# Token axis split at 256, the second token half of the first four weight groups first, in a hybrid decoder step on one core

## The chip, the cores and the metric

One Trainium2 chip, of which the kernel uses one core. The metric is the device time of one execution in microseconds (us). The core has TensorE (PE; its weight loads are PEld), VectorE (DVE), ScalarE (ACT), GpSimd (POOL) and SyncE (SP), which issues most of the DMAs. Each engine works its own instruction list in order and waits on semaphores.

## The reference

One layer of a hybrid decoder for a prompt of 512 tokens and 8 single-token samples (520 tokens in all), in float32:

```python
xn = rmsnorm(x, ln1_w)
z = xn @ w_in          # 1024 -> 3592 columns: q, k, v of attention; q, k, v, gate of mLSTM; 8 gate columns
attn = moba_attention(qa, k_all, v_all, q_start)     # 8 heads x 64; samples look at 1024 cached tokens
h, C, n, m = mlstm_chunkwise(qm, km, vm, i_pre, f_pre, C0, n0, m0)   # 4 heads x 128, matrix memory
mix = concat(attn, rmsnorm(h) * sigmoid(om))
x = x + mix @ w_out
x = x + square(relu(rmsnorm(x, ln2_w) @ w_up)) @ w_down              # 1024 -> 4096 -> 1024
y = rmsnorm(x, lnf_w)
```

Outputs are y, the new keys and values, and the mLSTM states, for prompt and samples.

## The kernel before

Activations lie transposed: features on the 128 partitions, the 520 tokens along the free axis. Each large product is made of three products of a high and a low part (`w_hi*x_hi + w_hi*x_lo + w_lo*x_hi`), summed in PSUM. A weight group is 128 output columns, 1024 deep. Its raw weights come by DMA into `raw` (two slots, a "unit" of two groups each, on SP's queue), ACT rounds them to `w_hi` (`split`, L1096), and DVE or POOL makes `w_lo` (`weight_lo`, L1103). Four groups fit in `w_hi` and `w_lo`. The token axis is cut in two halves of 260. A group and a half make one slot: 24 matmuls of 260 columns into one of three accumulators, which DVE evacuates (`evac_copy`, L1953) with the norm's factor `rstd1`. PE may start slot i only when slot i-3 has been evacuated. Slots 0 to 55 are the 28 input groups, 56 to 71 the 8 output groups; then follow 64 MLP groups.

What else has to be done is written by hand into the slots: `plan()` puts named tasks behind each slot, and each engine does its part of slot s and of the slot's tasks before it goes on to s+1. The tasks that matter here:

- `gates`: 24 matmuls for the gate columns of one half; `rows`, `rows_f`, `rows_sum`, `rows_max`, `rows_M`, `rows_s`, `rows_end`, `gcols` (slots 4 to 11): the running sums and maxima of the gates, on 4 partitions, most of it on DVE.
- `qs_tok`, `qb` (slots 8 and 9): the samples' queries, copied to all partitions as `Qb`.
- `score`: 32 chunks of cached keys. POOL multiplies a chunk of two pages with `Qb` (`prod`, two buffers, L1476), DVE reduces it to `S` (L1655). Chunk n stands in slot `10 + (2n+1)//3`, so in slots 10 to 31; key pages for chunk n+4 are issued on SP when chunk n is multiplied.
- `gate`, `mx_t`, `own`, `mx_b`, `p_sum`, `zsum` (slots 32 to 36), then `pv` from slot 37: the choice of blocks, softmax and the product with the cached values.
- `att_*`: prompt attention; `ml_*`: mLSTM. `ml_m` of head 0 stands in slot 27: ACT writes `mA`, POOL masks it (L1510).

At the start SP issues the four token tiles, unit 0, the gate columns, the page table, unit 1 and small loads, waits until the last token tile has been transposed and squared, issues 8 key pages (they lie over the token tiles), and only then unit 2. PE transposes all four tiles (32 transposes, L742), ACT and DVE split them at 512 columns (`act_hi` L1153, `act_lo` L1564), and slot 0 begins. POOL makes `w_lo` of groups 0 to 2, DVE of groups 3 to 19: group n in the even slot 2(n-3), ahead of that slot's evacuation.

Of the kernel before, what the change touches and what calls it, by code (L numbers as in the profile page):

```python
# [24 lines left out]
ALU = mybir.AluOpType  # L25
# [13 lines left out]
HALF = TOK // 2  # L39
# [34 lines left out]
HALVES = [(g, half) for g in range(N_IN) for half in range(2)]  # L74
# [11 lines left out]
def z_ready(g):  # L86

    return 2 * (g + 1)
# [19 lines left out]
def chunk_slot(n):  # L108

    return 10 + (2 * n + 1) // 3  # L110


def pv_slot(b):

    return 37 + 12 * b // 5
# [5 lines left out]
def plan():  # L121
# [6 lines left out]
    at(2, ("gates", 0))  # L128
    at(3, ("gates", 1))
    at(4, ("rows",))  # L130
    at(5, ("rows_f",))
    at(6, ("rows_sum",))
    at(7, ("rows_max",))
    at(8, ("qs_tok",), ("rows_M",))
    at(9, ("qb", 0), ("qb", 1), ("rows_s",))
    at(10, ("rows_end",))
    at(11, ("gcols",))
# [13 lines left out]
    at(32, ("gate",))  # L151
    at(33, ("mx_t",), ("own",))
    at(34, ("mx_b",))
    at(35, ("p_sum",))
    at(36, ("zsum",))
    for b in range(4):
        at(36, ("s_put", b))
# [9 lines left out]
    at(pv_slot(7) + 3, ("pv_end",))  # L167
    for h in range(MH):
# [12 lines left out]
        at((52, 54, 55, 55)[h], ("om_mix", h))  # L181
# [17 lines left out]
    for n in range(4 * NS):  # L199
        at(chunk_slot(n), ("score", *divmod(n, 4)))  # L200
        if n % 4 == 1 and n >= 5:
            at(chunk_slot(n), ("qb", n // 4 + 1)) if n // 4 + 1 < NS else None
    for t in range(4):
# [3 lines left out]
        "gates": 1, "gcols": 1, "qs_tok": 1, "qb": 1, "vs_tok": 1, "tokk": 1, "tokv": 1, "tokm": 2,  # L207
# [10 lines left out]
    for j in range(4, KT):  # L218
        job("xn", j)
    job("par2", 0)  # L220
    job("rstd1", 0)
    job("rstd1", 1)
# [29 lines left out]
def build(nc, x_prompt, x_sample, cache_k, cache_v, page_table, state_C, state_n, state_m, ln1_w, w_in,  # L252
# [4 lines left out]
    with ctx:  # L257
# [37 lines left out]
        mix, _ = place("mix", [P, N_IN, TOK], F32R, at=z_at)  # L295
        x_sq, _ = place("x_sq", [P, 2, TOK], at=z_slot(VA))
# [111 lines left out]
        s_pt_in = sem("pt_in")  # L408
        s_raw0 = sem("raw0")
# [17 lines left out]
        s_x_acc = sem("x_acc")  # L427
        s_x_lo = sem("x_lo")
# [130 lines left out]
        def _(sp):  # L559
            for i in range(NT):  # L560
                sp.dma_start(x_tok[:, i, :], x_prompt[0, i * P:(i + 1) * P, :]).then_inc(x_in[i], 16)
# [20 lines left out]
            unit(0)  # L582
# [3 lines left out]
            unit(1)  # L586
# [4 lines left out]
            full(sp, "xn", KT - 1)  # L591
            sp.wait_ge(s_x_sq_ok, NT + 1)
# [55 lines left out]
        def _(pe):  # L648
# [8 lines left out]
            def token_half(half):  # L657
                return slice(half * HALF, (half + 1) * HALF)

            def half_gemm(i, parts, k_ready=None):  # L660

                g, half = HALVES[i]
                pe.wait_ge(s_w_lo_ok, g + 1)
                if i >= 3:
                    pe.wait_ge(s_acc_evac, i - 2)
                for k in range(KT):
                    if k_ready is not None:
                        k_ready(k)
                    three(acc[:, i % 3, 0:HALF], g % WSLOTS, parts, token_half(half), k, k)

            def main(g, slot, side, parts, k_ready=None, between=None):
# [3 lines left out]
                def part(half, k):  # L675
                    three(acc[:, 2 * side + half, 0:HALF], slot, parts, token_half(half), k, k)
# [43 lines left out]

            pe.wait_ge(s_ident_ok, 3)

            for i in range(NT):
                pe.wait_ge(x_in[i], 16)
                if i == 2:

                    out = open_job(pe, "param", 0)
                    pe.wait_ge(s_ln1_in, 16)
                    pe.transpose(out[:, 0:KT], ln1_rows[:, :], ident[0:KT, 0:KT])
                    pe.wait_ge(x_in[NT], 16)  # L730
                    for j in range(KT):
                        mm = pe.transpose(out[:, 32 + j * NS:32 + (j + 1) * NS], x_s[:, j * P:(j + 1) * P],
                                          ident[0:NS, 0:NS])
                    done(mm)
                for j in range(KT):
                    if j == 7 and i < 2:
                        continue
                    out = acc[:, j, :] if j < 4 else bank("xn", j)
                    if j == 7 and i == 2:
                        open_job(pe, "xn", j)  # L740
                    for n in range(3) if j == 7 and i == 2 else (i,):
                        mm = pe.transpose(out[:, n * P:(n + 1) * P], x_tok[:, n, j * P:(j + 1) * P], ident[:, :])  # L742
                    if i == NT - 1 and j < 4:
                        mm.then_inc(s_x_acc, 1)
                    elif i == NT - 1:
                        done(mm)

            def task(name, *a):
                if name == "gates":
                    half, = a  # L750
                    if half == 0:
                        pe.wait_ge(s_wg_lo_ok, 2)
                    cols = token_half(half)
                    out = open_job(pe, "gates", half, 0)[:, 0:HALF]
# [14 lines left out]
                elif name == "qs_tok":  # L769
                    pe.wait_ge(s_acc_evac, z_ready(QA + 3))  # L770
# [263 lines left out]
            for i in range(N_HALVES):  # L1034
                if i == 0:
                    half_gemm(i, x_parts, x_split)
                    pe.wait_ge(s_xs_ok, 1)
                elif i < 2 * N_IN:
# [49 lines left out]
        def weight_hi(act, g, slot, r_slot, target):  # L1088

            act.wait_ge(raw_in[r_slot], target)  # L1090
# [17 lines left out]
        def _(act):  # L1108
# [34 lines left out]
            square_sum(1)  # L1143
            split(0)
            act.wait_ge(s_par_ok, 1)

            for j in range(KT):
                if j < 4:
                    act.wait_ge(s_x_acc, j + 1)
                    out = acc[:, j, :]  # L1150
                else:
                    out = full(act, "xn", j)
                act.activation(act_hi[:, j, 0:SEQ], out, ACT.Copy, scale=par[:, j:j + 1]).then_inc(s_xhi_ok, 1)  # L1153
                if j == 5:
                    split(1)
            square_sum(2)
            square_sum(NT - 1)
            split(2)
            free(act.activation(par[:, KT:20], full(act, "par2", 0)[:, 0:KT + MH], ACT.Copy), "par2", 0)
# [13 lines left out]
            def task(name, *a):  # L1173
                if name == "rows_f":
# [28 lines left out]
                elif name == "va_s":  # L1203
                    act.wait_ge(s_smp_out, 16)
# [223 lines left out]
        def _(pool):  # L1428
# [22 lines left out]
            for rows_split in (qs_split, M_split):  # L1451
                pool.memset(rows_split[:, :].bitcast(F32), 0.0).then_inc(s_sel_ok, 1)
            pool.memset(vm_tok[:, :, MD:MD + 1], 1.0).then_inc(s_vm_ones, 1)
            weight_lo(pool, 0, 0, 0)
            weight_lo(pool, 1, 1, 0)
            pool.wait_ge(s_x_ms_ok, 2)
            rsqrt(rs[:, 0:NT], P, NT).then_inc(s_x_rs_ok, 1)
            rsqrt(rs[0:NS, NT:NT + 1], NS, 1).then_inc(s_x_rs_ok, 1)
# [5 lines left out]
                               ALU.subtract).then_inc(s_wg_lo_ok, 1)  # L1464

# [51 lines left out]
            for s in range(N_HALVES):  # L1517
                n = s // 2 + AHEAD
                if s % 2 == 0 and n >= POOL_LO:
# [22 lines left out]
        def _(dve):  # L1542
# [16 lines left out]

            dve.wait_ge(s_par_ok, 1)  # L1560
            for j in range(KT):
                dve.wait_ge(s_xhi_ok, j + 1)
                out = acc[:, j, :] if j < 4 else full(dve, "xn", j)
                ins = dve.scalar_tensor_tensor(out=act_lo[:, j, 0:SEQ], in0=out, scalar=par[:, j:j + 1],  # L1564
                                               in1=act_hi[:, j, 0:SEQ].bitcast(F32), op0=ALU.mult, op1=ALU.subtract)
                if j < 4:
                    ins.then_inc(s_x_lo, 1)
                else:
                    free(ins, "xn", j)

# [6 lines left out]

            dve.wait_ge(s_x_sq_ok, NT + 1)
# [503 lines left out]
```

## Time and profile before

| what | us |
|---|---|
| median of 3 runs | 761.29 |
| lowest, highest | 758.21, 764.3 |
| profiled execution, its time | 758.09 |
| profiled execution, its span | 756.4 |

The span is that of the instructions; the time has 1.7 us around it. Working back from a row of the trace gives times within the span of the profiled execution, which is near the lowest of the three runs.

### The profile page before, as it was taken

To read this page: it belongs to the slowest core of one execution; us is meant where nothing else is said; L and a number is where in the kernel's file an instruction comes from. 1 tells how busy PE (TensorE), PEld (TensorE's weight loads), DVE (VectorE), ACT (ScalarE), POOL (GpSimd) and SP (SyncE) were. 2 spreads that over 40 slices of the span, in tenths; PEclk is the share of its full clock that TensorE was granted. 3 is DMA by queue.
4 is the path that set the end of the run, shared out by engine and by line. 5 is a ranking of instruction groups with operands and counts; after the bars stand their busy time and mean duration, and the time that the engine had idled before them with its cause. 6 is when DMAs were issued, how large, how long until landed. Compare 5 with 4: busy or idle time off the path is not lost.

```text
span 756.4 us, 14650 instructions
## 1 busy us (share of the span) xinstructions
PE 717.1 (95%) x5709; PEld 666.4 (88%) x5709; DVE 360.4 (48%) x649; ACT 254.9 (34%) x428; POOL 213.3 (28%) x154
## 2 busy tenths in 40 slices
PE   6999889698999999899999999999999999999995
PEld 5988778576968776599999999999999999999994
DVE  3279778768543346345334433334334333333333
ACT  6233645434452222215333311342223321233123
POOL 4207987743223253163222100220002200022001
PEclk9999999899999999999999999999999999999998
DMA  7627988654356868723123332232331331322102
GB/s 226 200 81 170 287 271 255 186 158 129 98 161 209 265 194 162 263 85 113 56 70 103 109 112 79 90 111 68 100 112 55 111 111 57 110 84 85 58 1 113
DMA packets 93732, 100.37 MB, mean 133 GB/s; under 512 B 5358, under 2 KB 75586, under 8 KB 93674
## 3 DMA queue, kind: packets, MB, share of 16 engines
q1 hardware_dynamic: 79670, 92.91, 39.8%
q10 hardware_dynamic: 14004, 6.67, 3.3%
q8 instruction: 39, 0.64, 0.4%
q14 instruction: 19, 0.16, 0.1%
HBM read 92.92 MB, written 6.64 MB: 132 GB/s over the span
## 4 chain that ended last, share of the span: by engine, by line
PE 74%; DVE 8%; issue 4%; DMA 4%; ACT 4%; POOL 4%; SPq 1%; ACTq 0%; POOLq 0%; DVEq 0%
PE acc L651 22%; PE acc L652 21%; PE acc L653 21%; DMA raw<-in_w_in_dram 2%; PE acc L932 2%; DMA kv<-in_cache_v_dram 2%; DVE w_lo L1103 2%; POOL prod L1476 1%; PE scr L982 1%; ACT w_hi L1096 1%; PE scr L863 1%; DVE S L1655 1%; PE scr L876 1%; PE scr L957 1%; DVE zT L1953 1%
## 5 line engine op out<-in xcount | busy, mean ns | idle before, releaser
L651 PE MATMUL acc<-act_hi,w_hi 128*128 128x260 f32 x960 | 277.8, 289 | 4.6 <-POOL w_lo L1103 2.6
L652 PE MATMUL acc<-act_lo,w_hi 128*128 128x260 f32 x960 | 273.1, 285 | 0.0
L653 PE MATMUL acc<-act_hi,w_lo 128*128 128x260 f32 x960 | 272.8, 284 | 0.0
L651 PEld LDWEIGHTS acc<-act_hi,w_hi 128*128 128x128 f32 x960 | 182.9, 191 | 12.4 <-issue 6.6
L653 PEld LDWEIGHTS acc<-act_hi,w_lo 128*128 128x128 f32 x960 | 183.0, 191 | 0.0
L652 PEld LDWEIGHTS acc<-act_lo,w_hi 128*128 128x128 f32 x960 | 183.0, 191 | 0.0
L1096 ACT ACTIVATE w_hi<-raw 128x1024 fp32r<-128x1024 f32 x100 | 105.2, 1053 | 185.0 <-PE acc L653 167.6
L1103 DVE TENSOR_TENSOR w_lo<-raw,w_hi 128x1024 fp32r<-128x1024 f32 x78 | 111.7, 1432 | 108.3 <-ACT w_hi L1096 107.9
L651 PE MATMUL acc<-h_hi,w_hi 128*128 128x260 f32 x512 | 144.6, 282 | 0.0
L652 PE MATMUL acc<-h_lo,w_hi 128*128 128x260 f32 x512 | 144.6, 282 | 0.0
L653 PE MATMUL acc<-h_hi,w_lo 128*128 128x260 f32 x512 | 144.4, 282 | 0.0
L1533 POOL TENSOR_TENSOR h_lo<-relu,h_hi 128x520 fp32r<-128x520 f32 x32 | 42.0, 1313 | 275.8 <-ACT h_hi L1404 275.8
L653 PEld LDWEIGHTS acc<-h_hi,w_lo 128*128 128x128 f32 x512 | 96.5, 188 | 0.0
L652 PEld LDWEIGHTS acc<-h_lo,w_hi 128*128 128x128 f32 x512 | 96.4, 188 | 0.0
L651 PEld LDWEIGHTS acc<-h_hi,w_hi 128*128 128x128 f32 x512 | 96.3, 188 | 0.0
L1476 POOL TENSOR_TENSOR prod<-kv,Qb 128x1024 f32<-128x1024 f32 x32 | 82.0, 2586 | 49.9 <-ACT Qb L1168 33.2
L1103 POOL TENSOR_TENSOR w_lo<-raw,w_hi 128x1024 fp32r<-128x1024 f32 x22 | 52.7, 2395 | 105.5 <-ACT w_hi L1096 105.5
L1973 DVE TENSOR_TENSOR xT<-acc,xT 128x260 f32<-128x260 f32 x64 | 27.1, 428 | 90.0 <-PE acc L653 90.0
L1403 ACT ACTIVATE relu<-relu 128x520 f32<-128x520 f32 x32 | 20.4, 639 | 123.5 <-DVE relu L2023 123.5
L1953 DVE TENSOR_TENSOR zT<-acc,rstd 128x260 f32<-128x260 f32 x56 | 23.5, 422 | 50.2 <-PE acc L653 47.4
L2023 DVE SCALAR_TENSOR_TENSOR relu<-acc,rstd 128x260 f32<-128x260 f32 x64 | 26.7, 422 | 39.1 <-PE acc L653 39.1
L1655 DVE TENSOR_REDUCE S<-prod 128x16 f32<-128x1024 f32 x32 | 38.3, 1209 | 8.4 <-POOL prod L1476 8.4
(294 smaller groups left out, 777.3 us busy)
## 6 DMA issues: line engine op xcount, KB each, us to landing
kv<-in_cache_k_dram SPq DMA_DIRECT2D x64, 256.0 KB, 3.2
kv<-in_cache_v_dram SPq DMA_DIRECT2D x64, 256.0 KB, 3.0
raw<-in_w_up_dram SPq DMA_DIRECT2D x16, 1024.0 KB, 5.4
raw<-in_w_down_dram SPq DMA_DIRECT2D x16, 1024.0 KB, 5.2
raw<-in_w_in_dram SPq DMA_DIRECT2D x8, 1024.0 KB, 6.2
raw<-in_w_in_dram SPq DMA_DIRECT2D x12, 512.0 KB, 5.4
x_tok<-in_x_prompt_dram SPq DMA_DIRECT2D x8, 512.0 KB, 5.2
raw<-in_w_out_dram SPq DMA_DIRECT2D x4, 1024.0 KB, 6.0
```

The lines of the kernel that those rows point to most:

```text
L651: pe.matmul(out, w_hi[:, slot, k, :], hi[k][:, cols], start=(n == 0), stop=False)
L652: pe.matmul(out, w_hi[:, slot, k, :], lo[k][:, cols], start=False, stop=False)
L653: mm = pe.matmul(out, w_lo[:, slot, k, :], hi[k][:, cols], start=False, stop=(n == KT - 1))
L1096: act.activation(w_hi[:, slot, :, :], raw[:, r_slot, :, side * P:(side + 1) * P], ACT.Copy)\
L1103: eng.tensor_tensor(w_lo[:, slot, :, :], raw[:, r_slot, :, side * P:(side + 1) * P], w_hi[:, slot, :, :].bitcast(F32), ALU.subtract).then_ ...
L1403: act.activation(relu2[:, t % 2, :], relu[:, t % 2, :], ACT.Square)
L1476: pool.tensor_tensor(prod[:, n % 2, :].rearrange("p (j n) -> p j n", j=2), kv[:, 2 * c:2 * c + 2, :], Qb[:, b % 2:b % 2 + 1, :].to_broadca ...
L1533: pool.tensor_tensor(h_lo[:, t, :], relu2[:, t % 2, :], h_hi[:, t, :].bitcast(F32), ALU.subtract).then_inc(s_hs_lo, 1)
L1655: dve.tensor_reduce(S[:, b, 2 * c:2 * c + 2, :].rearrange("p j h -> p (j h)"), prod[:, n % 2, :].rearrange("p (g d) -> p g d", d=AD), AX.X ...
L1953: dve.tensor_tensor(zT[:, g, cols], acc[:, i % 3, 0:HALF], rstd1[:, cols], ALU.mult)\
L1973: dve.tensor_tensor(x, acc[:, 2 * side + half, 0:HALF], x, ALU.add).then_inc(s_acc_evac, 1)
L2023: dve.scalar_tensor_tensor(out=relu[:, t % 2, cols], in0=acc[:, 2 * (t % 2) + half, 0:HALF], scalar=0.0, in1=rstd2[:, cols], op0=ALU.max, ...
```

## The change

The halves are now tokens 0 to 255 and tokens 256 to 519 (256 and 264 columns). The first eight slots are half 1 of groups 0 to 3, then half 0 of groups 0 to 3; from slot 8 on the order is as before. Token tiles 2 and 3 are loaded first, then group 0 and group 1 each in a DMA of its own, then tiles 0 and 1, then unit 1; gate columns, page table and small loads come behind it. Tiles 0 and 1 are transposed, split and squared as tasks of slots 1 and 2. In its first four slots PE waits for `w_lo` only after the 16 matmuls that need `w_hi` alone. The samples' square sum goes from ACT to DVE, the copy `va_smp` from DVE to ACT. The weights of groups 4 to 7 are split in slots 5 to 8; POOL makes `w_lo` of group 3 too. `qs_tok` and `qb` stand in slots 4 and 5, the `rows` tasks in slots 6 to 12, key scoring in slots 6 to 29, ahead of the `ml` tasks of the same slot, and `gate` to `zsum` and all `pv` one slot earlier.

```diff
-HALVES = [(g, half) for g in range(N_IN) for half in range(2)]
+HALVES = [(g, half) for half in (1, 0) for g in range(WSLOTS)]
+HALVES += [(g, half) for g in range(WSLOTS, N_IN) for half in range(2)]
...
+def token_half(half):
+    return slice(SPLIT_TOK, TOK) if half else slice(0, SPLIT_TOK)
...
+def split_at(s):
+
+    if s < 2 * WSLOTS + 1:
+        return s - 1 if s > WSLOTS else None
+    n = s // 2 + AHEAD
+    return n if s % 2 == 0 and n >= 2 * WSLOTS else None
...
 def chunk_slot(n):
 
-    return 10 + (2 * n + 1) // 3
+    return 6 + 3 * n // 4
...
 def pv_slot(b):
 
-    return 37 + 12 * b // 5
+    return 36 + 12 * b // 5
...
+    at(0, ("par2",), ("rstd", 1))
+    at(1, ("xn", 0), ("xn", 1))
+    at(2, ("xn", 2), ("xn", 3), ("square", 0), ("square", 1))
+    at(3, ("gates", 1), ("rstd", 0))
+    at(4, ("qs_tok",))
+    at(5, ("gates", 0), ("qb", 0), ("qb", 1))
+    at(6, ("rows_f",))
+    at(7, ("rows_sum",))
+    at(8, ("rows_max",))
+    at(9, ("rows_M",))
+    at(10, ("rows_s",))
+    at(11, ("rows_end",))
+    at(12, ("gcols",))
...
-            unit(0)
+            tokens(2)
+            tokens(3)
+            for n in range(2):
+                sp.dma_start(raw[:, 0, :, n * P:(n + 1) * P],
+                             w_in[0, :, COL[n] * P:(COL[n] + 1) * P].rearrange("(k p) n -> p k n", p=P))\
+                  .then_inc(raw_in[0] if n else s_raw_first, 16)
+            tokens(0)
+            tokens(1)
+            unit(1)
...
             sp.wait_ge(s_pt_in, 16)
-            full(sp, "xn", KT - 1)
-            sp.wait_ge(s_x_sq_ok, NT + 1)
+            full(sp, "xn", 3, 0)
+            sp.wait_ge(s_x_sq_ok, NT)
             for j in range(PAGES):
                 page(cache_k, 0, j)
...
+                if i < WSLOTS:
+                    hi, lo = parts
+                    pe.wait_ge(s_w_hi_ok, g + 1)
+                    for k in range(KT):
+                        pe.matmul(out, w_hi[:, g, k, :], hi[k][:, cols], start=(k == 0), stop=False)
+                        pe.matmul(out, w_hi[:, g, k, :], lo[k][:, cols], start=False, stop=False)
+                    pe.wait_ge(s_w_lo_ok, g + 1)
...
+            square_sum(2)
...
+            square_sum(3)
+            act.wait_ge(s_par_ok, 1)
+            x_hi(("x1", 0), 0, 1)
+            x_hi(("x1", 1), 1, 1)
             split(0)
+            x_hi(("x1", 2), 2, 1)
+            x_hi(("x1", 3), 3, 1)
+            split(1)
             split(2)
...
+                elif name == "xn":
+                    n, = a
+                    if n == 2:
+                        split(3)
+                    x_hi(("xn", n, 0), n, 0)
+                elif name == "square":
+                    square_sum(*a)
...
             for s in range(N_HALVES):
-                n = s // 2 + AHEAD
-                if s % 2 == 0 and n < POOL_LO:
-                    if n == AHEAD:
-                        dve.wait_ge(s_w_lo_ok, AHEAD)
+                n = split_at(s)
+                if n is not None and n < POOL_LO:
+                    if n == WSLOTS:
+                        dve.wait_ge(s_w_lo_ok, WSLOTS)
                     weight_lo(dve, n, n % WSLOTS, n // 2 % 2)
+                if s == slot_of(0, 1):
+                    rstd_to_cols(1)
+                if s == slot_of(0, 0):
+                    rstd_to_cols(0)
```

## Rows read from the trace of the kernel before

**Rows 1.** The page: busy time, share of the span and instructions of each engine

```profile
PE 717.1 (95%) x5709; PEld 666.4 (88%) x5709; DVE 360.4 (48%) x649; ACT 254.9 (34%) x428; POOL 213.3 (28%) x154
```

**Rows 2.** The waits of PE: engine, line waited for, total us, times, longest

```profile
PE scr L863 <- DVE pT_b L1901: 6.2, 1, 6.2
...
PE scr L903 <- DVE page_max L1799: 2.4, 1, 2.4
```

**Rows 3.** Busy time by stretch: PE, PEld, DVE, ACT, POOL, granted clock, DMA

```profile
140.00:160.00 20.00, 12.63 (x77) 10.64 (x75) 14.06 (x18) 2.11 (x3) 16.15 (x7) 0.83 0.61 186
...
384.00:756.00 372.00, 363.20 (x3041) 362.34 (x3040) 143.18 (x211) 107.56 (x149) 44.74 (x37) 0.99 0.27 88
```

**Rows 4.** The timeline of the start: start us, duration us, what, idle before it

```profile
2.71 0.59 SPq L573 DMA_DIRECT2D raw<-in_w_in_dram  x1
...
4.66 1.06 ACT L1135 ACTIVATE junk<-x_tok 128x1024 f32<-128x1024 f32 x1 [0.90 <-DMA x_tok<-in_x_prompt_dram]
...
6.29 1.06 PE L742 MATMUL acc<-ident,x_tok 128*128 128x128 f32 x4
...
12.04 1.06 ACT L1096 ACTIVATE w_hi<-raw 128x1024 fp32r<-128x1024 f32 x1 [1.63 <-DMA raw<-in_w_in_dram]
13.00 2.41 ACT L1153 ACTIVATE act_hi<-acc,par 128x512 fp32r<-128x512 f32 x4
13.18 2.35 POOL L1103 TENSOR_TENSOR w_lo<-raw,w_hi 128x1024 fp32r<-128x1024 f32 x1 [7.99 <-ACT w_hi L1096]
...
15.58 0.39 PE L651 MATMUL acc<-act_hi,w_hi 128*128 128x260 f32 x1 [2.59 <-POOL w_lo L1103]
```

**Rows 5.** The timeline of SP, and of ACT: key pages, units 2 and 3, groups 4 and 5

```profile
22.00 8.67 SPq L580 DMA_DIRECT2D kv<-in_cache_k_dram  x8
30.72 1.06 SPq L573 DMA_DIRECT2D raw<-in_w_in_dram  x2
...
38.12 2.01 ACT L1096 ACTIVATE w_hi<-raw 128x1024 fp32r<-128x1024 f32 x2 [12.46 <-DMA raw<-in_w_in_dram]
```

**Rows 6.** The timeline of DVE from group 4 to the evacuation of slot 13

```profile
39.21 1.22 DVE L1103 TENSOR_TENSOR w_lo<-raw,w_hi 128x1024 fp32r<-128x1024 f32 x1 [11.44 <-ACT w_hi L1096]
...
49.46 1.22 DVE L1103 TENSOR_TENSOR w_lo<-raw,w_hi 128x1024 fp32r<-128x1024 f32 x1 [2.84 <-ACT w_hi L1096]
...
59.62 2.02 DVE L1636 TENSOR_TENSOR s_rows<-rows,m_row 4x8 f32<-4x8 f32 x1
...
69.45 1.22 DVE L1655 TENSOR_REDUCE S<-prod 128x16 f32<-128x1024 f32 x1 [1.04 <-POOL prod L1476]
...
74.24 0.41 DVE L1953 TENSOR_TENSOR zT<-acc,rstd 128x260 f32<-128x260 f32 x1
```

**Rows 7.** The tile w_lo on DVE, by stretch: busy us (instructions)

```profile
38.00:64.00 26.00, 4.89 (x4) 1.00 0.33 103
66.00:160.00 94.00, 19.95 (x10) 0.95 0.83 239
```

**Rows 8.** The timeline of POOL, first key product and around head 0's masking

```profile
58.73 5.24 POOL L1476 TENSOR_TENSOR prod<-kv,Qb 128x1024 f32<-128x1024 f32 x2 [33.17 <-ACT Qb L1168]
...
138.34 1.04 POOL L1510 TENSOR_SCALAR_AFFINE_SELECT mA<-mA 128x128 f32<-128x128 f32 x4 [3.00 <-ACT mA L1281]
139.34 10.26 POOL L1476 TENSOR_TENSOR prod<-kv,Qb 128x1024 f32<-128x1024 f32 x4
```

**Rows 9.** PE by stretch: slots 0 and 1; slots 12, 13; slots 29, 30

```profile
15.58:23.73 8.15, 7.80 (x49) 0.79 0.08 21
65.09:71.12 6.03, 6.03 (x53) 1.00 0.90 116
149.54:156.97 7.43, 7.43 (x52) 0.79 0.91 300
```

**Rows 10.** The timeline of DVE in slots 25 and 27

```profile
129.41 2.24 DVE L1659 COPY va_smp<-zT 128x32 f32<-128x32 f32 x1
...
141.74 1.22 DVE L1655 TENSOR_REDUCE S<-prod 128x16 f32<-128x1024 f32 x1 [3.06 <-POOL prod L1476]
```

More of the change, by code:

```diff
@@ L38 @@
 TOK = SEQ + NS
-HALF = TOK // 2
+SPLIT_TOK = SEQ // 2
 AH, AD = 8, 64
@@ L150, in plan @@
     at(46, ("states", 4))
[L151 to L155, printed above, removed]
+    at(31, ("gate",))
+    at(32, ("mx_t",), ("own",))
+    at(33, ("mx_b",))
+    at(34, ("p_sum",))
+    at(35, ("zsum",))
     for b in range(4):
-        at(36, ("s_put", b))
+        at(35, ("s_put", b))
     for b in range(NS):
@@ L167, in plan @@
     at(pv_slot(7) + 3, ("pv_end",))
+    for n in range(4 * NS):
+        at(chunk_slot(n), ("score", *divmod(n, 4)))
+        if n % 4 == 1 and n >= 5:
+            at(chunk_slot(n), ("qb", n // 4 + 1)) if n // 4 + 1 < NS else None
     for h in range(MH):
@@ L217, in plan @@
     job("param", 0)
[L218 to L222, printed above, removed]
+    for n in range(4):
+        job("x1", n)
     for names in tasks:
@@ L559, in _, with tokens @@
         def _(sp):
-            for i in range(NT):
+            def tokens(i):
                 sp.dma_start(x_tok[:, i, :], x_prompt[0, i * P:(i + 1) * P, :]).then_inc(x_in[i], 16)
@@ L668, in half_gemm @@
                         k_ready(k)
-                    three(acc[:, i % 3, 0:HALF], g % WSLOTS, parts, token_half(half), k, k)
+                    three(out, g % WSLOTS, parts, cols, k, k)
             def main(g, slot, side, parts, k_ready=None, between=None):
@@ L675, in part @@
                 def part(half, k):
-                    three(acc[:, 2 * side + half, 0:HALF], slot, parts, token_half(half), k, k)
+                    three(acc[:, 2 * side + half, 0:width(half)], slot, parts, token_half(half), k, k)
                 def bank_free(half):
@@ L748, in task, with x_to_cols @@
-            def task(name, *a):
-                if name == "gates":
+            def x_to_cols(key, n, tiles):
+                out = open_job(pe, *key)
+                for j in (2 * n, 2 * n + 1):
+                    for c, i in enumerate(tiles):
+                        pe.wait_ge(x_in[i], 16)
+                        col = (j % 2) * SPLIT_TOK + c * P
+                        mm = pe.transpose(out[:, col:col + P], x_tok[:, i, j * P:(j + 1) * P], ident[:, :])
+                done(mm)
+            pe.wait_ge(s_ident_ok, 3)
@@ new lines, in _, with x_split_1 @@
+            out = open_job(pe, "param", 0)
+            pe.wait_ge(s_ln1_in, 16)
+            pe.transpose(out[:, 0:KT], ln1_rows[:, :], ident[0:KT, 0:KT])
+            pe.wait_ge(x_in[NT], 16)
+            for j in range(KT):
+                mm = pe.transpose(out[:, 32 + j * NS:32 + (j + 1) * NS], x_s[:, j * P:(j + 1) * P],
+                                  ident[0:NS, 0:NS])
+            done(mm)
+            for n in range(4):
+                x_to_cols(("x1", n), n, (2, 3))
+            def x_split_1(k):
+                evacuated(pe, "x1", k // 2)
@@ new lines, in x_split_0, with task @@
+            def x_split_0(k):
+                evacuated(pe, "xn", k // 2, 0)
+            def task(name, *a):
+                if name == "par2":
+                    pe.wait_ge(s_par_in, 32)
+                    out = open_job(pe, "par2", 0)
+                    done(pe.transpose(out[:, 0:KT + MH], par_rows[:, :], ident[0:KT + MH, 0:KT + MH]))
+                elif name == "rstd":
+                    half, = a
+                    pe.wait_ge(s_x_rs_ok, 2 if half else 3)
+                    out = open_job(pe, "rstd", half, 0)
+                    for n, c in enumerate((2, 3, NT) if half else (0, 1)):
+                        m = P if c < NT else NS
+                        mm = pe.matmul(out[:, n * P:n * P + m], every(rs[0:m, c:c + 1], m),
+                                       ident[0:m, 0:m], start=True, stop=True)
+                    done(mm)
+                elif name == "xn":
+                    n, = a
+                    x_to_cols(("xn", n, 0), n, (0, 1))
+                elif name == "gates":
@@ L750, in task @@
                     half, = a
-                    if half == 0:
+                    if half == 1:
                         pe.wait_ge(s_wg_lo_ok, 2)
+                    else:
+                        for k in range(KT):
+                            x_split_0(k)
                     cols = token_half(half)
-                    out = open_job(pe, "gates", half, 0)[:, 0:HALF]
+                    out = open_job(pe, "gates", half, 0)[:, 0:width(half)]
                     for k in range(KT):
@@ L1088, in weight_hi @@
         def weight_hi(act, g, slot, r_slot, target):
-            act.wait_ge(raw_in[r_slot], target)
+            if isinstance(g, int) and g == 0:
+                act.wait_ge(s_raw_first, 16)
+            else:
+                act.wait_ge(raw_in[r_slot], target)
             if not isinstance(g, int) or g >= G_MLP:
@@ L1558, in _ @@
                .then_inc(s_sel_ok, 1)
+            dve.wait_ge(x_in[NT], 16)
+            link(dve.tensor_tensor(xs_sq[:, :], x_s[:, :], x_s[:, :], ALU.mult))
+            link(dve.tensor_reduce(ss[0:NS, NT:NT + 1], xs_sq[:, :], AX.X, ALU.add))
             dve.wait_ge(s_par_ok, 1)
[L1561 to L1569, printed above, removed]
             evacuated(dve, "param", 0)
```

204 lines of the change are left out of this document (92 added, 112 removed).

## The prediction

> **What bounds the kernel now.** The page first: PE is busy 717.1 of 756.4 us, every other engine under half [rows 1]. The order of the MLP phase is not touched, and its 372 us are PE from end to end [rows 3]. So a gain can only come out of PE's idle and slowed time ahead of it. The list of PE's waits then shows that one wait is long, 6.2 us for a copy on DVE, and one of 2.4 for the block choice [rows 2]; the wait for the first tokens and weights is the third place: the first real matmul starts at 15.58 [rows 4]. The stretch 140 to 160 shows what the long wait costs beyond itself: PE busy 12.63 of 20 us at a granted clock of 0.83 [rows 3]. Slots 29 and 30 took 7.43 us at a clock of 0.79, slots 12 and 13 took 6.03 at 1.00 [rows 9], so 1.4 us more were lost to the lower level (1.2 GHz for part of the time) after PE had idled. From 6.03 us a slot is 3.0 us.
>
> **The first matmul.** Before, ACT had to wait for unit 0 until 12.04, behind four token tiles [rows 4]. Now ACT squares tile 2 from 4.66 to 5.9 (1.06 and the read of its sum), copies the parameters until 6.3, squares tile 3 until 7.6 (the tile that came second was in use at 6.29), and makes four pieces of `act_hi`. At 512 columns one takes 0.60 (2.41 for four); 256 columns lie between 0.30 and 0.60, I take 0.4, since fixed cost stays: 9.2. `w_hi` of group 0 takes 1.06: 10.2. Its weights need 1.5 MB of the 3.1 that had landed by 12.04, so they are there at about 7 to 8. First matmul 10.3 instead of 15.58, 5.3 earlier. POOL's `w_lo` (2.35) is ready at 12.6 and no longer holds the first 16 matmuls; slot 0 ends near 13.9. The samples' square sum costs DVE two operations over 1024 elements, about 1.2 each as the one that reduces 1024 [rows 6]; DVE has nothing else before the first `act_hi`, so I price it at nothing, 2.4 if that cover goes.
>
> **What is given back at once: transposes and the key pages.** Half of the transposes (16, four in 1.06 [rows 4]) move behind the first matmul. Slot 1 runs from about 14.7 to 17.7, eight transposes to 19.8, slot 2 to 22.8, eight more to 24.9. ACT then has its last pieces and two squares of 1.25: 28. SP waits for these squares before it issues key pages; with transposes somewhat faster I take 27.5, where before it was 22.00 [rows 5]; bounds 26 and 30 (the latter if the clock is low again, as in slots 0 and 1, 8.15 us at 0.79 [rows 9]). Unit 2 is queued behind the eight pages, and group 4's `w_hi` started 16.1 us after the first page (38.12 less 22.00). So it starts at 43.6, and `w_lo` of group 4 ends at 45.9, not 40.4. Slots 3 to 7, the gates (24 matmuls, as a slot), `qs_tok` and `qb` bring PE to slot 8 at about 47.8, so PE itself is not held. What is late is DVE: this `w_lo` stands ahead of its evacuation of slot 5.
>
> **The DVE chain to slot 13.** Before, from the end of `w_lo` of group 4 (40.4) to the end of slot 13's evacuation (74.65) it took 34.2 us [rows 6]. Taken away: idle time of 2.84 and 1.04; three evacuations of 0.41 (slots 2 to 4 are done by then); the gate products of one half, 0.8. Added: by the formula ten chunks instead of four stand in slots up to 12, six reductions of 1.22, 7.3. Then there is blocking. A `w_lo` on DVE took 1.22 where POOL was nearly idle (4.89 for 4) and 2.0 where POOL multiplied keys (19.95 for 10) [rows 7]; an operation on 32 elements took 2.02 just when the first two key products ran [rows 6, 8]. Four early `w_lo` and seven `rows` operations with two inputs in SBUF now stand beside key products. At 0.8 each that is 8.8, of which before had paid about 4 in `rows_s`; as the products stop whenever DVE is late, I take 2, bounds 0 and 9. Sum: 34.2 - 3.9 - 1.2 - 0.8 + 7.3 + 2 = 37.6, so slot 13 is evacuated at 83.5, 9 later. PE had slack there: slot 13 ended at 71.12 [rows 9], and slot 16, which must wait for this evacuation, had slots 14 and 15 (6.0) and tasks (I estimate 5) before it, so began near 82. It now begins at 83.5 at best and, since slots 14 and 15 are held in the same way, I take +4, bounds -2 and +9. The 5.3 us of the start are gone by then; what is kept is a lead of six chunks.
>
> **Slots 16 to 27.** Sixteen chunks where eighteen stood: 2.4 us less on DVE; and the copy of `va_smp`, 2.24 on DVE [rows 10], goes to ACT. PE waits only for part of that: -1.5, bounds 0 and -4.6.
>
> **Slots 27 to 32.** Here the lead pays. Before, seven chunks stood behind head 0's masking on POOL; POOL waited 3.00 for ACT's `mA` and then had four products back to back, 10.26 [rows 8]. DVE waited 3.06 for one of them [rows 10] with the copy behind it for which PE waited 6.2 [rows 2]. Now chunks 28 and 29 stand ahead of the masking and only 30 and 31 behind it. Wait and slow clock make 7.6; I take -7, bounds 0 and -9. The 2.4 for the block choice stays: `gate` and `mx_t` are still one slot apart.
>
> **The rest.** The cached values one slot earlier meet fewer state stores: -0.5, bounds -2 and +2. Evacuations and matmuls of 256 and 264 columns make 520 as before, so I price them at nothing; the MLP phase too.
>
> **Sum.** +4 - 1.5 - 7 - 0.5 = -5.0. The profiled execution took 758.1, so 753.1 by it; it lies 3.2 under the median of the three runs, 761.29, to which the forecast is made: 756.
>
> **The rivals.** (a) The start is kept: pages at 26, no added blocking, slot 16 two us earlier, then -1.5, -7.6 and -0.5, together -12: 749. For it: POOL was idle for 33.17 us before the first product [rows 8], and DVE's chain had 3.9 idle. Against it: DVE's sum above. (b) The wait of 6.2 is not removed but meets the next thing late, the `mA` products on DVE, which now stand behind chunk 30, itself behind the masking: +4 - 1.5 - 0.5 and nothing back, 763. For it: POOL's wait for ACT is untouched. (c) Slower: on DVE and POOL the early chunks and the `rows` chain take turns. The eleven operations each wait for the rest of a product, on average half of 2.4, 13 us less the 4 paid before, 9 at slot 16; a low clock costs 1.4 more, and of the later 7 only 2 come back, since PE arrives there with DVE late: +9 + 1.4 - 1.5 - 2 = +7, 768. It decides once slot 13's evacuation ends after about 88. For it: rows 7; against it: two product buffers let POOL run only two chunks ahead of DVE.
>
> The Trainium skill has a rule for (c): SBUF — State Buffer, section "Who interferes with whom", says that a DVE instruction with two SBUF inputs and a GpSimd instruction that reads SBUF exclude each other, the later one waiting until the first is through. The trace agrees in direction: the doubled `w_lo` and the 2.02 us for 32 elements. Taken strictly it makes every one of those operations wait, which is rival (c), 768, where my sum takes 2 us. The same section lets a reduction, with its single input, run beside POOL, and the reductions of 1.22 [rows 6] bear that out.
>
> **Chances.** Forecast 0.45, (a) 0.20, (b) 0.14, (c) 0.21. Leaving out the outer parts of (a) and (c), the range is 746 to 768. One per cent, about what a measurement of this kernel can tell from no change, is 7.6 us: faster than 753.7 is (a) and the lower third of the forecast, 0.34; slower than 768.9 the most of (c) with its spread, 0.20; between them 0.46.
>
> **What would show it.** First L651 matmul near 10.3 (wrong if over 12). First key page near 27.5, group 4's `w_hi` near 43.6. First key product near 42 instead of 58.73. `w_lo` on DVE near 2 us already before 60. Slot 13's evacuation between 79 and 88. After slot 27 no PE wait over 3 us for the copy into `pT_b`, and granted clock 1.00 there. The forecast is wrong if the early waits of PE (slots 8 to 14) add up to over 14 us, or if the pages start before 25 and DVE keeps pace.

## The result, and the profile after

The changed kernel takes 777.10 us (median of 4 runs, 776.04 to 779.11), the kernel before 760.18 (4 runs): ratio 1.022, interval 1.019 to 1.024. It is 2.2% slower, where 756 was forecast with a range up to 768. The profiled execution took 779.11 us, 777.4 of them span. It is the slowest of its four, and the profiled execution of the kernel before lies just under the fastest of its four, so the spans lie 21.0 us apart where the medians lie 16.9 apart: rows show where the time went, ratios how much it is.

The page of the changed kernel, busy line (it answers to [rows 1]):

```profile
PE 722.6 (93%) x5709; PEld 671.8 (86%) x5709; DVE 367.2 (47%) x658; ACT 254.3 (33%) x435; POOL 219.6 (28%) x156
```

The number of PE's instructions is the same as before. The span is 21.0 us longer and PE's busy time only 5.5, so 15.5 us are idle time of PE. The waits of PE name where (engine, what for, total, times, longest):

```profile
PE acc L676 <- DVE zT L2031: 10.5, 4, 5.2
PE scr L921 <- DVE pT_b L1979: 4.5, 1, 4.5
...
PE scr L967 <- DVE nmax L1961: 3.5, 1, 3.5
...
PE scr L774 <- DMA x_s<-in_x_sample_dram: 2.4, 1, 2.4
```

Against [rows 2] the first row is new: a half group waits for the evacuation (`zT`) of an earlier one, on DVE. The wait for `pT_b` is 4.5 instead of 6.2. In place of the 2.4 for the block choice stands one of 3.5. By stretch (us, then busy time of PE, PEld, DVE, ACT and POOL, granted clock, DMA share, GB/s):

```profile
40.00:60.00 20.00, 14.44 (x106) 13.40 (x106) 14.68 (x15) 7.43 (x9) 11.54 (x4) 0.89 0.69 221
60.00:80.00 20.00, 11.83 (x84) 10.88 (x83) 19.79 (x17) 3.46 (x4) 10.57 (x5) 0.84 0.45 146
...
180.00:200.00 20.00, 15.64 (x90) 13.15 (x89) 14.29 (x42) 6.40 (x16) 2.96 (x5) 0.83 0.25 66
```

Before, PE was busy 17.61 and 20.00 us in the first two of these stretches, at a granted clock of 1.00; DVE, with 19.79 of 20 us, is what it now waits for. Both stretches also lost some clock (0.89 and 0.84) after PE had idled: slots 10 and 13 took 4.8 us each instead of 3.1 and 3.0.

Where the time came from can be followed slot by slot. A slot is 24 matmuls of the query groups, so every 24th of these matmuls in the record begins one (there are 200, slots 0 to 199):

```
first matmul of slot   0      9      13     16     28     29     33     60     198
before (us)          15.58  53.74  68.08  82.26 136.27 149.54 175.47 333.39 738.65
after (us)           11.82  49.81  79.30  97.92 151.92 164.03 194.18 352.50 759.60
difference            -3.8   -3.9  +11.2  +15.7  +15.7  +14.5  +18.7  +19.1  +21.0
```

Between slots 9 and 16, 20 us are lost. All that comes later changes this by 5.

SP's and ACT's timelines, which answer to [rows 5] (start, duration, what, idle before it):

```profile
29.39 8.13 SPq L598 DMA_DIRECT2D kv<-in_cache_k_dram  x8
37.56 12.13 SPq L591 DMA_DIRECT2D raw<-in_w_in_dram  x3
```

```profile
43.58 1.06 ACT L1147 ACTIVATE w_hi<-raw 128x1024 fp32r<-128x1024 f32 x1 [8.45 <-DMA raw<-in_w_in_dram]
44.54 1.07 ACT L1216 ACTIVATE Qb<-scr 128x512 f32<-128x512 f32 x2
```

Group 4's `w_hi` came at 43.58, as forecast (43.6). The failure is in DVE's timeline from there to slot 13's evacuation, the answer to [rows 6]:

```profile
44.74 1.23 DVE L1154 TENSOR_TENSOR w_lo<-raw,w_hi 128x1024 fp32r<-128x1024 f32 x1 [8.83 <-ACT w_hi L1147]
45.88 0.42 DVE L2031 TENSOR_TENSOR zT<-acc,rstd 128x256 f32<-128x256 f32 x1
...
47.08 2.22 DVE L1154 TENSOR_TENSOR w_lo<-raw,w_hi 128x1024 fp32r<-128x1024 f32 x1
...
49.67 2.14 DVE L1685 TENSOR_SCALAR rows<-rows,bias_f 4x520 f32<-4x520 f32 x1
...
56.13 2.10 DVE L1154 TENSOR_TENSOR w_lo<-raw,w_hi 128x1024 fp32r<-128x1024 f32 x1 [0.38 <-ACT w_hi L1147]
58.16 0.41 DVE L2031 TENSOR_TENSOR zT<-acc,rstd 128x256 f32<-128x256 f32 x1
58.49 2.52 DVE L1693 SCALAR_TENSOR_TENSOR rows<-rows 4x520 f32<-4x520 f32 x1
...
62.30 1.22 DVE L1734 TENSOR_REDUCE S<-prod 128x16 f32<-128x1024 f32 x1
...
64.90 2.53 DVE L1699 TENSOR_TENSOR rows<-rows 4x512 f32<-4x512 f32 x1
...
70.19 2.58 DVE L1706 CAST M_split<-rows 4x512 fp32r<-4x512 f32 x1
...
76.38 2.54 DVE L1154 TENSOR_TENSOR w_lo<-raw,w_hi 128x1024 fp32r<-128x1024 f32 x1
...
79.17 1.98 DVE L1715 TENSOR_TENSOR s_rows<-rows,m_row 4x8 f32<-4x8 f32 x1
...
84.21 2.15 DVE L1154 TENSOR_TENSOR w_lo<-raw,w_hi 128x1024 fp32r<-128x1024 f32 x1
...
89.78 0.42 DVE L2031 TENSOR_TENSOR zT<-acc,rstd 128x264 f32<-128x264 f32 x1
```

DVE has almost no gap in 44 us (0.38 and 0.72), and nine operations are too long: each is held up by a product on POOL, which is called blocking here, and the lock in the expectations. Before, the TENSOR_SCALAR took 0.47 us, the next two `rows` operations 0.68 and 0.67, the CAST 0.42; `w_lo` takes 1.22 when it runs free, the 32 elements of `s_rows` 0.15. What the nine have too much is 1.00 + 0.88 + 1.32 + 0.93 for `w_lo`, 1.67 + 1.84 + 1.86 + 2.16 for `rows`, and 1.83 for `s_rows`: 13.5 us. The reductions `S` beside the same products stay at 1.20 to 1.22. Before, three operations of the same stretch were held, the 2.02 of [rows 6] and these two, by 1.87, 2.17 and 1.04, 5.1 us in all:

```profile
61.67 2.32 DVE L1637 TENSOR_TENSOR m_s<-s_rows,rows 4x8 f32<-4x8 f32 x1
...
70.59 2.26 DVE L1103 TENSOR_TENSOR w_lo<-raw,w_hi 128x1024 fp32r<-128x1024 f32 x1
```

POOL's timeline, for [rows 8]:

```profile
45.20 6.33 POOL L1538 TENSOR_TENSOR prod<-kv,Qb 128x1024 f32<-128x1024 f32 x2 [15.87 <-ACT Qb L1216]
54.79 5.67 POOL L1538 TENSOR_TENSOR prod<-kv,Qb 128x1024 f32<-128x1024 f32 x2 [3.26 <-DVE S L1734]
63.69 3.20 POOL L1538 TENSOR_TENSOR prod<-kv,Qb 128x1024 f32<-128x1024 f32 x1 [3.22 <-DVE S L1734]
70.10 2.39 POOL L1538 TENSOR_TENSOR prod<-kv,Qb 128x1024 f32<-128x1024 f32 x1 [3.21 <-DVE S L1734]
```

Three times POOL waited about 3.2 us for a reduction, then started a product, and the next DVE operation of a kind that doesn't run beside it stood still. How long shows in the ends: the TENSOR_SCALAR ends 0.28 us after the product beside it (51.81 and 51.53), the CAST 0.28 after its own (72.77 and 72.49), the other two `rows` operations 0.55 and 0.54 after theirs. So each waited for the rest of a product. It goes the other way too: where DVE had begun first, as with the `w_lo` of 1.22 at 63.43, the product took 3.20 us instead of 2.39. The two engines take turns.

### The profile page after: what moved, and what is told of

It reads as the page before. It is cut to its first block, busy times and chain, and to the rows that moved or that the text cites. A ratio compares the mean times of both kernels' runs of the same rounds, so it can differ in the third digit from the quotient of the medians.

```text
span 777.4 us, 14680 instructions
## 1 busy us (share of the span) xinstructions
PE 722.6 (93%) x5709; PEld 671.8 (86%) x5709; DVE 367.2 (47%) x658; ACT 254.3 (33%) x435; POOL 219.6 (28%) x156
## 4 chain that ended last, share of the span: by engine, by line
PE 75%; DVE 9%; ACT 3%; issue 2%; POOL 2%; DMA 2%; ACTq 0%; SPq 0%; POOLq 0%; DVEq 0%
PE acc L676 22%; PE acc L677 21%; PE acc L678 21%; PE acc L990 2%; DVE w_lo L1154 2%; DMA kv<-in_cache_v_dram 2%; DVE S L1734 1%; PE scr L1040 1%; PE scr L921 1%; PE scr L934 1%; POOL prod L1538 1%; ACT w_hi L1147 1%; PE scr L1015 1%; PE scr L1028 1%; POOL sm_t L1490 1%
## 5 line engine op out<-in xcount | busy, mean ns | idle before, releaser
L676 PE MATMUL acc<-act_hi,w_hi 128*128 128x256 f32 (+1 forms) x928 | 271.3, 292 | 11.1 <-DVE zT L2031 10.5
L677 PE MATMUL acc<-act_lo,w_hi 128*128 128x256 f32 (+1 forms) x928 | 265.9, 287 | 0.0
L678 PE MATMUL acc<-act_hi,w_lo 128*128 128x256 f32 (+1 forms) x928 | 265.4, 286 | 0.0
L676 PE MATMUL acc<-h_hi,w_hi 128*128 128x264 f32 (+1 forms) x512 | 145.0, 283 | 0.0
L677 PE MATMUL acc<-h_lo,w_hi 128*128 128x264 f32 (+1 forms) x512 | 144.7, 283 | 0.0
L678 PE MATMUL acc<-h_hi,w_lo 128*128 128x264 f32 (+1 forms) x512 | 144.6, 282 | 0.0
L2051 DVE TENSOR_TENSOR xT<-acc,xT 128x256 f32<-128x256 f32 x64 | 27.2, 429 | 90.2 <-PE acc L678 90.2
L2031 DVE TENSOR_TENSOR zT<-acc,rstd 128x264 f32<-128x264 f32 (+1 forms) x56 | 23.7, 424 | 62.4 <-PE acc L678 55.9
L2105 DVE SCALAR_TENSOR_TENSOR relu<-acc,rstd 128x256 f32<-128x256 f32 x64 | 26.7, 422 | 40.0 <-PE acc L678 40.0
L676 PE MATMUL acc<-mix,w_hi 128*128 128x264 f32 (+1 forms) x128 | 38.1, 298 | 3.6 <-DVE mix L1997 3.2
```

Source lines behind the costliest of these rows:

```text
L676: pe.matmul(out, w_hi[:, slot, k, :], hi[k][:, cols], start=(n == 0), stop=False)
L677: pe.matmul(out, w_hi[:, slot, k, :], lo[k][:, cols], start=False, stop=False)
L678: mm = pe.matmul(out, w_lo[:, slot, k, :], hi[k][:, cols], start=False, stop=(n == KT - 1))
L2031: dve.tensor_tensor(zT[:, g, cols], acc[:, i % 3, 0:width(half)], rstd1[:, cols], ALU.mult)\
L2051: dve.tensor_tensor(x, acc[:, 2 * side + half, 0:width(half)], x, ALU.add).then_inc(s_acc_evac, 1)
L2105: dve.scalar_tensor_tensor(out=relu[:, t % 2, cols], in0=acc[:, 2 * (t % 2) + half, 0:width(half)], scalar=0.0, in1=rstd2[:, cols], op0=AL ...
```

## The experiments

Ratios are to the kernel before, timed beside it on the same chip, so two experiments are compared by their ratios; 0.1% is 0.76 us. "Slot 13" is the start of that evacuation (before 74.24, changed 89.78).

**1. The widths alone**, in the kernel before:

```diff
-HALF = TOK // 2
+SPLIT_TOK = SEQ // 2          # halves of 256 and 264 columns everywhere
```

> The kernel before with halves of 256 and 264 columns instead of 260 and 260; order of slots, loads and tasks as before. In the MLP phase of the changed kernel matmuls follow each other after 118.7 ns at 256 columns and 121.4 at 264, mean 120.07, where 260 columns had 119.50. Over 4800 matmuls that is 2.7 us. Theory that the widths cost it: +2 to +3.5 us, ratio 1.003 to 1.005. Theory of my prediction (the sum of columns is the same, so no cost): within 0.5 us.

Measured: 761.04 against 759.14 us, ratio 1.003 (1.001 to 1.005). The price shows where PE never waits, in a window of the MLP phase, kernel before first, then this one:

```profile
400.00:740.00 340.00, 340.00 (x2851) 1.00 0.26 84
```

```profile
400.00:740.00 340.00, 340.00 (x2838) 1.00 0.26 84
```

13 matmuls fewer in 340 us, 0.5%. The starts of matmuls lie 119.50 ns apart at 260 columns, 118.77 at 256 and 121.31 at 264, whose mean is 120.04. So the price is real, some 2 us, and about a tenth of the loss.

**2. The new start without the early scoring**, in the changed kernel:

```diff
-    return 6 + 3 * n // 4
+    return 10 + (2 * n + 1) // 3      # chunk_slot as before
```

and the score tasks behind those of the heads, `gate` to `zsum` and `pv` in their old slots.

> The changed kernel with its new start (slots 0 to 9, loads, rows tasks, qs and qb as changed), but key scoring back in slots 10 to 31 and behind the ml tasks of its slot, and gate to zsum and pv in their old slots. Theory A (the early key products and reductions on top of the rows chain make the loss): slot 16 starts within 3 us of before's 82.3 and the whole is 755 to 763. Theory B (the late key pages and unit 2 make it, w_lo of group 4 ends at 46.0 instead of 40.4): slot 16 stays 6 or more late, the whole is over 767.

Measured: 762.76 us, ratio 1.005 (1.003 to 1.006). Slot 13 at 75.54, slot 16 at 83.56 (before 82.26). So the new start, with the late unit 2 in it, does no harm worth the name beyond the widths, and no good either: its 5 us are gone by slot 13. Of the 2.2%, 1.7 (13 us) go with the early scoring.

**3. The later tasks as before**, with the early scoring kept:

```diff
-    at(31, ("gate",))
+    at(32, ("gate",))                 # and each task after it, pv too, one slot later
```

and the score tasks behind those of the heads.

> The changed kernel with early scoring (slots 6 to 29), but scoring behind the ml tasks of its slot, and gate to zsum and pv one slot later, as before. Theory A: the loss of 15.7 us at slot 16 stays; only the loss between slots 32 and 33 (4.4 us more than before: the block choice and head 0's ml_o share slot 31 on DVE) goes: 770 to 774. Theory C (the order behind slot 27 is the main cause): 765 or less.

Measured: 776.88 us, ratio 1.024 (1.022 to 1.025), which can't be told from the changed kernel; the 770 to 774 expected were missed. Inside it both edits show: slot 33 starts 13.9 us later than before, not 18.7, so the +4.2 between slots 29 and 33 goes with the block choice in slot 31; but the step from slot 28 to 29 takes 14.7 us instead of 12.1, since the masks are again ahead of the products.

**4. Units 2 and 3 ahead of the key pages** on SP, in the changed kernel:

```diff
+            unit(2)
+            unit(3)
             sp.wait_ge(s_pt_in, 16)
             full(sp, "xn", 3, 0)
```

> The changed kernel, but SP issues units 2 and 3 ahead of the first eight key pages, so that w_lo of groups 4 and 5 isn't held by them; all else as changed. Theory B: w_lo of group 4 ends some 8 us earlier (below 38.5 instead of 46), slot 16 starts 6 to 8 us earlier, the whole is 769 to 772. Theory A: DVE's chain stays full from the first key product on (which waits for the queries' slot, not for the weights), gain 3 us or less, 774 to 778.

Measured: 770.18 us, ratio 1.014 (1.011 to 1.016), by the ratios 6 us less than the changed kernel. DVE's timeline:

```profile
35.48 1.23 DVE L1156 TENSOR_TENSOR w_lo<-raw,w_hi 128x1024 fp32r<-128x1024 f32 x1 [0.27 <-ACT w_hi L1149]
36.62 0.42 DVE L2033 TENSOR_TENSOR zT<-acc,rstd 128x256 f32<-128x256 f32 x1
```

Group 4's `w_lo` starts 9.3 us earlier than in the changed kernel, and slot 13 is evacuated at 84.55, 5.2 earlier.

**5 and 6. Products that read nothing.** In the changed kernel and, as a control, in the one before, POOL's product is replaced by memsets of nearly its length. They leave out the product of pages and queries, so the samples' scores aren't computed; every wait and every reduction stays:

```diff
-                    pool.tensor_tensor(prod[:, n % 2, :]..., kv page, Qb, ...)
+                    for part, w in enumerate((2 * AW, 2 * AW)):
+                        pool.memset(prod[:, n % 2, 0:w], 1.0).then_inc(s_pool_chain, 1)
+                        pool.wait_ge(s_pool_chain, 5 + 2 * n + part + 1)
+                    pool.memset(prod[:, n % 2, 0:384], 1.0)
```

> The changed kernel; POOL's product of a key chunk with the queries is left out and three memsets of the same output, together about 2.4 us as the product, stand in its place, in the same queue places and behind the same waits. They read nothing of SBUF; the reductions on DVE stay. (The scores of the samples are left out by it.) Lock theory: DVE's two-input and copy operations no longer take 2.0 to 3.2 us, w_lo is 1.2 throughout, slot 13 is evacuated at 77 to 81 instead of 90.2, and the whole is 760 to 766. Load theory (the early reductions and the chain of waits themselves fill DVE): slot 13 not before 86, the whole 772 to 777.

> The same exchange in the kernel before, as control: what the lock costs there. Lock theory: w_lo 1.2 throughout, the 6.2 us wait for the copy into pT_b shrinks, 2 to 8 us faster than before, so less than the changed kernel gains by it. If it gains as much as the changed kernel (12 us or more), the lock isn't what the change made worse.

Measured: 758.54 us in the changed kernel, ratio 1.001 (0.998 to 1.003), and 754.08 in the one before, 0.994 (0.992 to 0.996). By the ratios the same edit gives 16 us in the one and 4.6 in the other; the first is more than was expected. What is left between these two kernels, some 5 us, isn't blocking by the products. The late unit 2, the widths, the six more reductions on DVE and the earlier block choice may have a share in it; no run divides it. In DVE's timeline of the fifth kernel, beside POOL's memsets:

```profile
46.49 1.23 DVE L1154 TENSOR_TENSOR w_lo<-raw,w_hi 128x1024 fp32r<-128x1024 f32 x1
...
48.09 1.12 DVE L1686 TENSOR_SCALAR rows<-rows,bias_f 4x520 f32<-4x520 f32 x1
...
55.01 0.68 DVE L1694 SCALAR_TENSOR_TENSOR rows<-rows 4x520 f32<-4x520 f32 x1
...
62.99 1.11 DVE L1707 CAST M_split<-rows 4x512 fp32r<-4x512 f32 x1
...
69.19 0.14 DVE L1716 TENSOR_TENSOR s_rows<-rows,m_row 4x8 f32<-4x8 f32 x1
...
77.64 0.42 DVE L2032 TENSOR_TENSOR zT<-acc,rstd 128x264 f32<-128x264 f32 x1
```

The operations have their free length again, but for the TENSOR_SCALAR and the CAST with 1.1, and the same order of work reaches slot 13 12.1 us earlier. Group 4's `w_lo` ends 0.6 us earlier as well (45.37), so the chain behind it is 11.5 shorter; the rows gave 13.5, less the two remainders of 0.65 and 0.69, 12.2. That is the blocking, by itself, to within 0.7 us. The wait for `pT_b` falls to 1.0, and slot 29 follows slot 28 after 7.3 us instead of 12.1 (before 13.3): here is the later gain that the forecast counted on, in a kernel in which DVE isn't held.

**7 and 8. The start kept, the scoring late.** The changed kernel with the edits of 2 and 4 together; in the eighth also 260 columns in both halves but for slots 0 to 7:

```diff
+def edge(g):
+    return SPLIT_TOK if isinstance(g, int) and g < WSLOTS else TOK // 2
```

> The changed kernel with units 2 and 3 ahead of the key pages, key scoring in slots 10 to 31 behind the ml tasks, and gate, softmax and pv in their old slots: the new start kept, its two costs that the earlier runs showed taken out, widths of 256 and 264 kept. If the late unit still costs when scoring is late: slot 16 starts at 78 to 80 instead of 83.6, the whole 756 to 759. If what follows absorbs it (the wait for pT_b after slot 28 grows by what PE arrives earlier): 760 to 763.

> As e7_combo, but the halves are 256 and 264 columns only in the eight slots of groups 0 to 3; all later slots and the MLP have 260 and 260. Width theory: 1.8 to 2.7 us less than e7_combo. No-cost theory: the same within 0.5.

Measured: 756.67 us, ratio 0.996 (0.994 to 0.999), and 755.52, 0.995 (0.993 to 0.997). Slot 13 is at 69.78 and 70.06: with unit 2 ahead of the pages the start's lead lives. By the ratios, unit 2 gave 6 us here over experiment 2, as it did in experiment 4. The widths make no difference here that these runs can tell. What is won over the kernel before is small; the wait for `pT_b` is still 6.2 and 6.1.

**9. The order inside a slot.** The eighth kernel with one edit, which the change also had: a slot's score tasks ahead of the heads' tasks:

```diff
+    for n in range(4 * NS):
+        at(chunk_slot(n), ("score", *divmod(n, 4)))
     for h in range(MH):
...
-    for n in range(4 * NS):
-        at(chunk_slot(n), ("score", *divmod(n, 4)))
```

> e8_combo260 with the scoring task ahead of the ml tasks of its slot, as in the changed kernel; scoring stays in slots 10 to 31. Before this, slots 28 to 29 took 13.3 us in the kernel before, 12.1 in the changed one (scoring first) and 14.7 with early scoring behind the ml tasks. If the order matters by itself: the wait for the copy into pT_b (6.1 us) shrinks by 1 to 3, the whole is 752 to 755. If the wait comes from DVE's queue in any order: 755 to 757.

Measured: 748.57 us, ratio 0.987 (0.982 to 0.992), the fastest of all, some 7 us under the eighth, and below the 752 to 755 expected. POOL's timeline, first the eighth kernel:

```profile
132.62 1.03 POOL L1578 TENSOR_SCALAR_AFFINE_SELECT mA<-mA 128x128 f32<-128x128 f32 x4 [4.35 <-ACT mA L1346]
133.62 10.26 POOL L1544 TENSOR_TENSOR prod<-kv,Qb 128x1024 f32<-128x1024 f32 x4
```

and then the ninth:

```profile
128.55 5.54 POOL L1544 TENSOR_TENSOR prod<-kv,Qb 128x1024 f32<-128x1024 f32 x2 [0.15 <-DMA kv<-in_cache_k_dram]
134.05 1.02 POOL L1578 TENSOR_SCALAR_AFFINE_SELECT mA<-mA 128x128 f32<-128x128 f32 x4
135.05 8.01 POOL L1544 TENSOR_TENSOR prod<-kv,Qb 128x1024 f32<-128x1024 f32 x3
```

Two products fill the 4.35 us in which POOL had waited for `mA`; the wait for `pT_b` falls from 6.1 to 2.9. The stretch that answers to [rows 3], eighth and then ninth kernel:

```profile
140.00:160.00 20.00, 16.03 (x106) 14.09 (x107) 13.73 (x23) 4.36 (x12) 11.93 (x5) 0.83 0.70 206
```

```profile
140.00:160.00 20.00, 18.55 (x149) 16.11 (x148) 14.91 (x35) 6.62 (x17) 10.14 (x6) 1.00 0.61 184
```

With the wait of 2.9 us PE's granted clock in this stretch stays at 1.00, with the one of 6.1 it is 0.83. Slot 29 takes 3.10 us instead of 5.04.

**10. Scoring from the eighth half group on**, in the eighth kernel:

```diff
-    return 10 + (2 * n + 1) // 3
+    return 8 + 3 * n // 4
```

> e8_combo260 with scoring in slots 8 to 31 (8 + 3n//4), so half way to the changed kernel's slot 6: four chunks more stand in slots 8 to 12, beside rows_max, rows_M and rows_s. Lock theory: DVE's operations there are blocked again, slot 13's evacuation ends 5 to 9 us later than in e8_combo260 (70.5), the whole is 758 to 763, slower than before the change in part. Rival (that only the late unit 2 and the tail made early scoring costly): 753 to 756.

Measured: 766.70 us, ratio 1.008 (1.005 to 1.011). Slot 13 at 78.42, 8.4 us after the eighth kernel, as the lock theory had it; the whole is slower than its 758 to 763. Even with a start that is 5 us ahead, scoring beside the `rows` chain turns a gain of 0.5% into a loss of 0.8%.

**11. The order alone**, in the kernel before (the edit of the ninth):

> The kernel before with one edit alone: in a slot that has both, the key chunk's tasks stand ahead of head 0's tasks, as the changed kernel has them. If the order is what pays between slots 27 and 32 (theory), chunk 28's reduction and its two products run before the masks of mA, PE's wait for the copy into pT_b falls from 6.2 to about 3, slots 28 to 29 take about 9 instead of 13 us, and the whole is 3 to 7 us faster: ratio 0.991 to 0.996. If the gain of the eighth kernel's successor needed the new start with it (rival), PE's wait stays above 5 and the ratio is within 0.998 to 1.002.

Measured: 756.81 us against 759.89, ratio 0.996 (0.995 to 0.997). `pT_b` is waited for 4.3 us, and slot 29 follows slot 28 after 11.4 us, not 13.3. So the order pays without the new start, by 3 us, though the step to slot 29 was expected at about 9. With the new start it paid 7. There slots 29 and 34, which ran at a low clock in the eighth kernel, run at full speed; in the eleventh, slot 29 still takes 4.97 us. Why the lead matters for this is only argued: the masks come at 140.60 in the eleventh and at 134.05 in the ninth.

## Why the prediction was wrong

The step that failed is the term for blocking in "The DVE chain to slot 13": "as the products stop whenever DVE is late, I take 2, bounds 0 and 9". It measured 8.4. With it failed the discount behind it, "PE had slack there", by which 9 us on DVE were to become +4 on PE: they became +15.7. Of the 26.0 us between the forecast's -5.0 and the +21.0 of the two traces, 11.7 lie at slot 16, 1.5 in slots 16 to 27, 5.8 at slots 28 and 29 and 7.0 behind them.

- **The first matmul** came at 11.82, not 10.3: PE waited 2.4 us for the samples' tokens, which the forecast didn't look at. In the other kernels with this start it came at 10.3 to 11.1, so the sum was right in kind.
- **The key pages** started at 29.39 (27.5, bounds 26 and 30), group 4's `w_hi` at 43.58 (43.6), the end of its `w_lo` was 45.97 (45.9). That the last two fit so well is luck: from the first page to `w_hi` it took 14.2 us, not 16.1, which made up for the late pages. And though the forecast saw that DVE would be late by this `w_lo`, it took PE's slack to cover it. Experiment 4 shows that it didn't: 6 us of the loss were this queue on SP. The first key product came at 45.20, not near 42.
- **The blocking.** From the end of `w_lo` to the end of slot 13's evacuation it took 44.2 us (45.97 to 90.20); the forecast was 37.6. Blocking was 13.5 us in the changed kernel and 5.1 before, so 8.4 were added, not 2, near the upper bound of 9. That is 6.4 of the 6.6 by which the chain came out longer; the other terms were right together. The eleven meetings at 0.8 were nine at 1.5. The argument for 2 was the error: products stop when DVE is late, but each reduction that ends releases one, and it starts just ahead of DVE's next operation. So turn-taking made a meeting likelier here, not rarer. And two of the nine, the TENSOR_SCALAR and the CAST, have a single input and weren't priced at all.
- **The slack of PE.** "PE had slack there" turned +9 into +4 at slot 16. It began 15.7 us later, as much as slot 13's evacuation (15.5). The slots before were held in the same way, and the start's 5 us could not count twice. DVE's chain was critical from slot 5's evacuation on (slots 10 and 13 began at 58.62 and 79.30, each 0.05 us after the end of the evacuation three slots before), and the whole lateness came through. This is rival (c): its mechanism, and the point from which it decides (evacuation after 88; it was 90.2), were right. Its 768 was still too low: its +9 at slot 16 were 15.7, and it had nothing for what was lost behind slot 29.
- **Slots 16 to 27**, -1.5: measured 0 (+15.7 at both ends).
- **Slots 27 to 32**, -7: measured -1.2 from slot 28 to 29. DVE was held there too, by one more product:

```profile
158.67 3.21 DVE L1154 TENSOR_TENSOR w_lo<-raw,w_hi 128x1024 fp32r<-128x1024 f32 x1
161.80 0.41 DVE L2031 TENSOR_TENSOR zT<-acc,rstd 128x256 f32<-128x256 f32 x1
162.13 0.54 DVE L1979 COPY pT_b<-scr 128x384 f32<-128x384 f32 x1
```

  This `w_lo`, 2.0 us too long, stands in front of the copy for which PE waits. Experiments 9 and 11 show where the gain lies: in the order of tasks within a slot, which the forecast didn't tell from the lead of six chunks.
- **The rest**, -0.5: measured +6.5 from slot 29 on. Of it +4.2 fall between slots 29 and 33, since the block choice now shares slot 31 with head 0's output on DVE. "`gate` and `mx_t` are still one slot apart" looked at their distance, not at what else stands in the slot. Moved back (experiment 3), the 4.8 at slot 33 return.
- **The widths**, priced at nothing: 0.3%, 2 us, most of it in the MLP phase (slot 60 to slot 198: +1.9).
- The rule quoted with rival (c) was the better forecast. The trace agrees: of DVE's operations that began beside a running product, those with two inputs in SBUF waited, and the reductions did not. The Trainium skill, SBUF — State Buffer, "Who interferes with whom", also counts `cast` and `tensor_scalar` among those that can take the shared ports. The rows of 2.14 and 2.58 agree, and the forecast had left them out.

## What to carry to other kernels

When a DVE operation is put beside a GpSimd one that reads SBUF, price each meeting at the rest of the GpSimd instruction, not at a share of it, and do so for casts and tensor-scalar operations too; where the GpSimd work is released by DVE's own results, take every operation behind such a release as met. Ask for each transfer that moves which engine's queue it feeds, and follow the chain of that engine instead of asking whether PE is held. Test the parts of a change one at a time: here one of them (tasks that release GpSimd ahead of tasks that wait for it) was worth 3 to 7 us and lay hidden under one that cost 13.

## What the runs showed of the hardware that had not been expected

- A write-only GpSimd instruction holds up some DVE operations as well: beside memsets of 0.95 us the TENSOR_SCALAR took 1.12 us (0.47 free) and the CAST 1.11 (0.42 free). Both ended 0.28 us after the memset, just as they had after a product. So these two were held by less because the memset was shorter than the product, not because it read nothing. Beside the same memsets `w_lo` and the other two-input operations kept their free length (1.23, 0.68, 0.14).
- Starts of matmuls lie 118.8 ns apart at 256 columns, 119.5 at 260 and 121.3 at 264. The step from 256 to 260 is 0.7 ns and the next 1.8, so two halves of 260 cost less than 256 and 264.
